# Expert weight ring of a DeltaNet/MLA/MoE trunk: each 1 MB matrix in two transfers of 64 partitions with 8192 B rows

## The reference

```
def swiglu(x, wg, wu, wd):
    return (jax.nn.silu(x @ wg) * (x @ wu)) @ wd

# per MoE layer: 512 tokens, 64 experts, 8 per token (sigmoid scores, best 4 of 8 groups)
# y = shared swiglu(x) + sum over the token's 8 experts of w_e * swiglu(x; gate[e], up[e], down[e])
# gate[e], up[e]: 1024 x 256 float32 (1 MB each), down[e]: 256 x 1024 float32 (1 MB)
```

## Time and profile before

| what | value |
|---|---|
| runs before, median (lowest to highest) | 2580.89 us (2578.11 to 2583.52), 3 runs |
| profiled execution | 2584.4 us, its span 2582.7 us |
| mean granted TensorE clock | 0.936 |
| PE, DVE, ACT, POOL busy | 2317.7, 1811.2, 1357.8, 825.4 us |
| HBM read, written | 495.31 MB, 50.14 MB |

### The profile page before, as it was taken

How to read it: one execution, slowest core, us unless ns; L and a number is a source line. 1 busy time by engine, 2 the same in 40 slices (tenths; PEclk the granted TensorE clock), 3 DMA queues, 4 the chain that set the end, 5 groups by cost and what they waited for, 6 DMA issues and landing times. The chain is left out here.

```text
span 2582.7 us, 39490 instructions
## 1 busy us (share of the span) xinstructions
PE 2317.7 (90%) x11685; PEld 1862.2 (72%) x11685; DVE 1811.2 (70%) x2757; ACT 1357.8 (53%) x2066; POOL 825.4 (32%) x467
## 2 busy tenths in 40 slices
PE   8989788878979999999999399998799999999992
PEld 6867777667668888888887265576588888888872
DVE  3759555545269999999997222433589999999993
ACT  3332211220258777777777122312377777888882
POOL 0000332210025555555555000000145555555551
PEclk9999899989789999999999599797899999999996
DMA  5321000000279999999998411013599999999993
GB/s 182 98 66 53 1 1 1 1 18 33 102 268 338 339 346 346 342 341 343 343 346 261 160 41 49 1 37 115 181 337 349 349 353 343 348 341 346 336 326 96
DMA packets 174997, 534.46 MB, mean 207 GB/s; under 512 B 23009, under 2 KB 52673, under 8 KB 174657
## 3 DMA queue, kind: packets, MB, share of 16 engines
q1 hardware_dynamic: 148720, 461.82, 49.2%
q0 software_dynamic: 23456, 67.14, 11.3%
q10 hardware_dynamic: 2736, 4.38, 0.5%
HBM read 495.31 MB, written 50.14 MB: 211 GB/s over the span
## 5 line engine op out<-in xcount | busy, mean ns | idle before, releaser
L1206 DVE TENSOR_TENSOR gu_l<-ring,gu_h 128x1024 fp32r<-128x1024 f32 x512 | 728.8, 1461 | 17.3 <-ACT gu_h L1107 6.3
L1107 ACT CAST gu_h<-ring 128x1024 fp32r<-128x1024 f32 x512 | 518.8, 1077 | 15.8 <-DVE y L1223 9.7
L1329 POOL TENSOR_TENSOR down_l<-ring,down_h 128x1024 fp32r<-128x1024 f32 x130 | 316.2, 2432 | 488.3 <-ACT down_h L1115 485.0
L1045 PE MATMUL bank<-gu_h,xgT_l 128*128 128x512 f32 x1024 | 411.8, 402 | 0.0
L1115 ACT CAST down_h<-ring 128x1024 fp32r<-128x1024 f32 x260 | 259.5, 1046 | 284.3 <-PE bank L1076 276.9
L1047 PE MATMUL bank<-gu_h,xgT_h 128*128 128x512 f32 x1024 | 400.8, 391 | 0.0
L1046 PE MATMUL bank<-gu_l,xgT_h 128*128 128x512 f32 x1024 | 399.8, 390 | 0.0
L1339 POOL DMA_INDIRECT xg<-h_rows,list_idx x128 | 142.6, 1114 | 705.4 <-issue 485.9
L1351 POOL DMA_INDIRECT moe_sum<-y,out_idx x128 | 272.7, 2130 | 66.4 <-issue 66.4
L1074 PE MATMUL bank<-down_h,hmT_l 128*128 128x512 f32 x544 | 231.6, 426 | 19.8 <-POOL down_l L1329 19.8
L1047 PEld LDWEIGHTS bank<-gu_h,xgT_h 128*128 128x128 f32 x1024 | 192.4, 188 | 42.4
(11 more groups left out here) (292 smaller groups left out, 3867.1 us busy)
## 6 DMA issues: line engine op xcount, KB each, us to landing
ring<-in_moe_w_gate SPq DMA_DIRECT2D x256, 512.0 KB
ring<-in_moe_w_up SPq DMA_DIRECT2D x256, 512.0 KB
ring<-in_moe_w_down SPq DMA_DIRECT2D x256, 512.0 KB
ring<-in_a_w_in SPq DMA_DIRECT2D x32, 512.0 KB
ring<-in_a_w_out SPq DMA_DIRECT2D x8, 512.0 KB
h_rows<-y SPq DMA_DIRECT2D x8, 512.0 KB, 2.6
moe_sum<-y ACTq DMA_DIRECT2D x8, 512.0 KB, 5.2
resid<-moe_sum SPq DMA_DIRECT2D x8, 512.0 KB, 6.2
```

Source lines behind the costliest of these rows:

```text
L1045: nc.tensor.matmul(out, lhsT=xl, rhs=wh, start=k == 0, stop=False)
L1107: nc.scalar.copy(gu_h[:, c, :, :], gate_up_cols(gate_slot, c * CH // 2, CH // 2)).then_inc(gu_hi.sem, 1)
L1206: nc.vector.tensor_tensor(gu_l[:, c, :, :], gate_up_cols(gate_slot, c * CH // 2, CH // 2), gu_h[:, c, :, :].bitcast(F32), ALU.subtract).th ...
L1329: nc.gpsimd.tensor_tensor(down_l[:, 1, :], ring[:, down_slot, CH:2 * CH], down_h[:, 1, :].bitcast(F32), ALU.subtract).then_inc(down_lo.sem, 1)
```

## The change

Unit 0 of an expert is now the whole of gate and unit 1 the whole of up; down stays whole. Each of the three is loaded by two transfers, partitions 0 to 63 and 64 to 127, with the full row of 8192 B per partition, where before each transfer had 128 partitions with 4096 B. The shared expert's units are changed alike. As a chunk of gate and up now reads both slots, ACT waits for both units before its first chunk, and both slots are released when all four chunks are used. `gate_up_cols` takes its columns from two neighbouring slots. Bytes, number of transfers and all compute instructions are the same.

```diff
--- before.py
+++ after.py
@@ -202,14 +202,13 @@
             gu = CH_GU * E * layer
             down = CH_DOWN * (1 + E) * layer + CH_DOWN
             gate, up = flat(a["moe_ws_gate"][layer]), flat(a["moe_ws_up"][layer])
-            for j in range(2):
-                half = slice(j * HALF, (j + 1) * HALF)
-                units[n + j] = ((gate[:, half], up[:, half]), None, gu_ready, gu_shared)
+            units[n] = ((gate[0:P // 2, :], gate[P // 2:P, :]), None, gu_ready, gu_shared)
+            units[n + 1] = ((up[0:P // 2, :], up[P // 2:P, :]), None, gu_ready, gu_shared)
             units[n + 2] = (flat(a["moe_ws_down"][layer]), None, down_lo, down)
             n += 3
             UNIT_EXPERT[layer] = n
             for e in range(E):
-                units[n] = (None, None, gu_lo, gu + CH_GU * e + CH_GU // 2)
+                units[n] = (None, None, gu_lo, gu + CH_GU * (e + 1))
                 units[n + 1] = (None, None, gu_lo, gu + CH_GU * (e + 1))
                 units[n + 2] = (None, None, down_lo, down + CH_DOWN * (e + 1))
                 n += 3
@@ -246,7 +245,7 @@
                     _, _, used, value = units[n - RING]
                     sp.wait_ge(used.sem, value)
                 if isinstance(view, tuple):
-                    parts = [(ring[:, n % RING, j * HALF:(j + 1) * HALF], view[j]) for j in range(2)]
+                    parts = [(ring[j * (P // 2):(j + 1) * (P // 2), n % RING, :], view[j]) for j in range(2)]
                 elif width:
                     dst, k = unit_cols(n), view.shape[1] // 2
                     parts = [(dst[:, :k, :], view[:, :k, :]), (dst[:, k:, :], view[:, k:, :])]
@@ -993,8 +992,7 @@
 
             def gate_up_cols(slot, c0, width):
 
-                j, c0 = divmod(c0, HALF)
-                return ring[:, slot + j, :].rearrange("p (g c) -> p g c", g=2)[:, :, c0:c0 + width]
+                return ring[:, slot:slot + 2, c0:c0 + width]
 
             def bump(pool):
 
@@ -1100,8 +1098,9 @@
 
                 gate_slot, _, arrived = item_units(r, i, False)
                 for c in parts:
-                    if c % 2 == 0:
-                        arrived(act, c // 2)
+                    if c == 0:
+                        arrived(act, 0)
+                        arrived(act, 1)
                     if r >= 1:
                         act.wait_ge(gu_ready.sem, gu_ready.base + CH_GU * (TT + r - 1) + c + 1 + 4 * CH_GU * i)
                     nc.scalar.copy(gu_h[:, c, :, :], gate_up_cols(gate_slot, c * CH // 2, CH // 2)).then_inc(gu_hi.sem, 1)
@@ -1387,9 +1386,8 @@
                         _, _, used, value = units[n - RING]
                         sp.wait_ge(used.sem, value + 4 * (CH_GU if used is gu_lo else CH_DOWN) * i)
                         for h in range(2):
-
-                            w, c0 = (weights[h], j * HALF) if j < 2 else (weights[2], h * HALF)
-                            sp.dma_start(ring[:, n % RING, h * HALF:(h + 1) * HALF], w[bass.ds(r + 4 * i, 1), :, c0:c0 + HALF].rearrange("e p c -> (e p) c")).then_inc(slot_loaded[n % RING].sem, 16)
+                            rows = slice(h * (P // 2), (h + 1) * (P // 2))
+                            sp.dma_start(ring[rows, n % RING, :], weights[j][bass.ds(r + 4 * i, 1), rows, :].rearrange("e p c -> (e p) c")).then_inc(slot_loaded[n % RING].sem, 16)
 
                     def load_gate_up(r, i):
                         load_unit(r, i, 0)
```

## The result

The changed kernel takes **3150.5 us** (median of 4 runs, 3103.77 to 3163.38) against 2582.2 us of the kernel before on the same chip: 568 us more. The ratio is 1.2104, 95% interval [1.1962, 1.2245]; it is made from the undisturbed runs alone (3145.88 and 3103.77 us of the changed kernel), which puts the loss at 543 us, and from here on differences between variants are read from such ratios where two exist. The runs of the changed kernel scatter over 2%, those before over 0.2%, so a difference of less than about 40 us from the changed kernel, the half-width of that interval, says little; the profiled execution took 3155.12 us.

A forecast was written before the change was run, and what follows sets the result against it. PE was taken to set the pace with DMA close behind; halved weight rate made each expert 17.22 us against 10.67, +6.55 us over 124 periods, +812 on 2584.4, said as 3400 us, range 2850 to 3680 us.

The forecast's parts named there:

- Bytes and compute cost nothing: Expert loops: six 512 KB transfers per expert before and after, same casts, subtractions and matmuls; no cost by themselves.
- Rows of 8192 B, 0: Weight transfers: longer rows at most remove a cost per packet, gain 0 to 18 us, taken as 0.
- 64 partitions, half of the rate, taken as 210 GB/s: Weight loads: writing 64 partitions at a time halves the undisturbed 420 GB/s to 210, ends 182 and 420.
- The sum, 14.98 + 2.24 = 17.22 us: Per expert: weights at 210 GB/s plus gathers and scatters as now, against 10.67 us; +6.55 us, 124 times, +812 us.
- Later release, nothing while DMA is the bound: Ring slots: the first slot is released 2.67 us later and the first cast waits for 2 MB; no cost at 17 us per expert.
- rival D: Expert loops: rate not halved, but later slot release adds at most 2.67 us per period, +331; 2750 us at half; chance 0.06.
- The shared expert's units, left out: Shared expert's gate and up: two units per layer, 5 us more each layer if uncovered, not counted.
- A: Weight loads: engines drift apart so the halves partly overlap, 13.48 us per expert, +348, 2930 us; chance 0.17.
- B: PE in the expert loops: its clock falls to half speed and it becomes the bound, +1280, 3865 us; chance 0.05.
- C: Weight loads: gathers are slow for another reason, 64-partition transfers run at 420 GB/s, time stays 2584 us; chance 0.07.
- E: Expert loops: longer rows free DMA time, rate not halved, PE's idle time goes, 18 us faster, 2566 us; chance 0.05.

The follow-up runs named there:

- the bare stream: Separate kernel with weight loads into the ring only, no compute or indirect traffic, transfer shapes varied: 128 x 8192 B 423 GB/s, 64-partition halves 219.
- the single transfers: Changed kernel with one transfer of 128 partitions x 8192 B per unit in place of two of 64 partitions: 2603.91 us, ratio 1.0094.

## Why the prediction was right, and where it was off

The direction and the range were right (2850 to 3680 us, measured 3150.5); the predicted 3400 us is 8% too high by the median, 9% by the ratio (about 3125 us). By its steps:

1. *Bytes and compute cost nothing*: right. The stages outside the loops kept their length (445 us between the loops hold 366.4 us of PE work before and 366.9 after); the loop holds the loss.
2. *Rows of 8192 B, 0*: right. The bare rate rises from 410 to 423 GB/s, but in the kernel it was not gained (2603.91 us).
3. *64 partitions, half of the rate, taken as 210 GB/s*: right as a mechanism, 5% low in size. The bare stream, which has nothing but the shape of its transfers, gave 219, and the loop fills SBUF at 222. The halves overlap a little, which the step had put at nothing. The rows that it rested on carry less than it drew from them: the windows of the earlier trace rows are low ones (182 to 236, where the average is 275), so that their mean of 217 met the stream's 219 was luck, and the drop goes away with 128-row gathers that write the same partitions. "Writing to partitions 0 to 63 alone slows the engines" was right for the weights, and is not what the gathers showed. The weights came in at 205 GB/s of wall time. The 196 GB/s that the prediction set beside its 210 lies under every stream of halves measured here (205 to 251).
4. *The sum, 14.98 + 2.24 = 17.22 us*: **this is the step that was off.** It added q0's 2.24 us of engine time in full to a term that was no longer engine time. With 64-partition loads the limit is the rate at which SBUF is filled, and the engines' time leaves room. Of the 2.24 us, the scatter-adds come to 15.36 - 15.22 = 0.14 us per expert by the traces, not clear of the spread of the runs, and the gathers to 15.36 - 14.00 = 1.36 us, most of it their bytes. The loop is 3.404 MB at 222 GB/s: 14.20 us for the weights and 1.16 for the gathers. So of the 17.22 - 15.36 = 1.86 us by which the period was too long, 0.8 come from the weights' rate (step 3) and 1.1 from q0. Times 124 the 1.86 us are 231 us; the forecast was 250 us above the median.
5. *Later release, nothing while DMA is the bound*: nothing speaks against it. Where DMA is not the bound, whole units and the later release together cost 9 us (2592.11), less than a thirtieth of rival D's upper bound of 331 us.
6. *The shared expert's units, left out*: the stages outside the loops show nothing of it.

Rivals. A, partial overlap: its 2930 us was not reached, but a part of it is there. Overlap gives the 7% of 219 over 205 GB/s, and about 0.8 of the 3.74 us between the forecast's 17.22 and A's 13.48 us; with runs half as long the kernel came to 2960.67 us. The reason that the prediction gave against A, that engines meet again at each transfer, holds only in part, and the 6% that it set against A came out here as 7% from alternating halves on one queue and 22% from two queues (251 against 205). B: the granted clock fell to 0.89 and PE was busy 78% of the loop, 11.9 of 15.36 us per expert, so it is not the bound. C fell with the bare stream, E with the single transfers.

What the forecast named as marks held, except two sizes: the slices show 232 to 248 GB/s and not 190 to 225 (205 of weights and 34 of indirect bytes), between the forecast's mark and the 250 to 300 that was A's, and PE's share is 78%, not 60%, because the period was shorter and the clock lower.

## What to carry to other kernels

Split a load by columns, not by partitions: 128 x 4096 B and 64 x 8192 B are the same bytes per transfer and moved at 410 and 219 GB/s in the bare stream. Read the GB/s beside the DMA share, since a share of 1.0 occurs at 205 and at 423 GB/s. And when a change moves the bound from one resource to another, write the ledger anew in the units of the new one, rather than adding the old one's remaining terms: here bytes written into SBUF replaced engine time, and traffic that only reads SBUF became nearly free. Last, windows of 2 us picked from a trace can be extremes: compare the average of all events of a kind before a rate is read from three of them.

## What I had not expected of the hardware

Top and bottom halves on two queues reach only 251 GB/s, 15% over one queue, although transfers for both halves are then in flight together. The fastest form alone (one transfer of 128 x 8192 B, 423 GB/s) is 12 us slower in the kernel than two transfers of 128 x 4096 B at 410. And writing a gather as 128 rows gains 9 us where the weights use all partitions and costs about 100 us where they do not.
